# A two-block transformer on one core: the sine-table work of layer 0 split and moved, and the filler matmuls of the mix loop moved from step 15 to step 14

## Chip, core and metric

One Trainium2 chip, one of its cores. The metric is device microseconds from start to end of one execution, the median of several executions. The engines are TensorE (PE), VectorE (DVE), ScalarE (ACT), GpSimd (POOL) and the DMA queues that SyncE (SP) and ScalarE issue.

## What is computed

Two small transformer stacks run one after the other on the same 512 tokens of width 1024. The change touches only the first one, whose two layers are:

```python
for l in range(DEPTH):                      # DEPTH = 2
    h = rms_norm(x, g_mix_norm[l]);  z = h @ w_in[l]
    q_lat, kv_lat, k_rope = z[..., :256], z[..., 256:384], z[..., 384:416]
    uv, pin = z[..., 416:928], z[..., 928:]
    a  = mla_mixer(q_lat, kv_lat, k_rope, positions, ...)   # 4 heads, causal softmax, rotary part of 32
    gm = sgu_mixer(uv, ...);  po = pool_mixer(pin, ...)
    mix = concat([rms_norm(a), rms_norm(gm), rms_norm(po)])
    x = x + mix @ w_out[l]
    h = rms_norm(x, g_ffn_norm[l])
    x = x + (silu(h @ w_gate[l]) * (h @ w_up[l])) @ w_down[l]

def apply_rope(x, positions):
    ang = positions * inv_freq              # reduced by multiples of 2 pi in the kernel
    cos, sin = cos(ang), sin(ang)
    return concat([x1 * cos - x2 * sin, x2 * cos + x1 * sin])
```

The second stack has a gated convolution layer and a dilated-attention layer, each with a squared-ReLU MLP and a gate at the end; it uses the same sine and cosine tables (the upper 64 rows hold its frequencies).

## The kernel before

Everything is held transposed, with channels on the 128 partitions and the 512 tokens along the free axis. Weights stream from memory in 225 slabs of 128 x 2048 floats. SP loads a slab into one of two stage buffers, POOL splits it into a high part and a low part, and PE multiplies in three products (high by high, low by high, high by low: lines 665 to 667), so that the result has nearly the precision of fp32. The program is a list of phases written out by hand; within a phase the order on each engine is the order of the code, and semaphores tie the engines together.

A phase called mix is one layer of the first stack up to `w_out`. PE's order at its start, with the names that matter:

- Slab 0 and slab 1 give PSUM banks 0 and 1 (query latents) and banks 2 and 3 (key-value latents, raw rotary keys). In layer 0 the sum of squares of `x` is also made there; ACT takes its root (`root`) and DVE its reciprocal, `rstd` (`finish_norm`).
- `turn_rstd` transposes `rstd` into bank 6 (line 921). DVE copies one column of each block out (`columns_of_rstd`, line 2039) and so frees bank 6.
- Slab 2 is multiplied with the tokens on the partitions, one quarter `c` of the tokens at a time, 24 matmuls each. Inside `c == 1`, PE takes bank 6 (`take(p, 6)`) and makes four narrow sums (`narrow_sum`, line 940): 8 small matmuls each that add ACT's squares of the latents (`narrow_square`, line 1547) over the channels.
- Slab 3 raises the latents to queries, keys and values, and from there a long chain of small operations on DVE leads to the first scores.

In layer 0, DVE also prepares the rotary tables between `finish_norm` and `columns_of_rstd`: `angles` multiplies positions by frequencies, finds the nearest multiple of 2 pi and subtracts it in four parts. ACT's `tables` waits for it (`angle_ready`), then takes sine, absolute value and sine again; it stands in ACT's order ahead of the square of bank 2. Layer 1 has neither.

Later in the phase is the mix loop: 16 steps, four heads by four blocks of 128 query tokens. At loop turn `t`, PE makes the scores of step `t` and transposes the probabilities of step `r = t - 2` (line 1100), for which DVE has multiplied by the reciprocal of the row sum (line 2237). `busy_work` puts matmuls whose result nobody reads (line 710) ahead of the wait at steps 10 and 15. After the loop come the first six products of `w_out` (`out_part`), the last head's values (line 1067), and the spreading of a norm (`spread_norm`, line 718), which goes on to the rest of the `w_out` products.

Of the kernel before, what the change touches and what calls it, by code (L numbers as in the profile page):

```python
# [142 lines left out]
def two_pi_parts():  # L143

    parts, rest = [], 2 * math.pi
    for _ in range(3):
        unit = 2.0 ** (math.floor(math.log2(rest)) - 7)
        parts.append(math.floor(rest / unit) * unit)
        rest -= parts[-1]
    return parts + [rest]  # L150
# [29 lines left out]
def build(nc, a):  # L180

    ctx = ExitStack()
    with ctx:
# [194 lines left out]
        def col(name, i=0):  # L378
            c = COLUMN_AT[name] + i
            return cols[:, c:c + 1]  # L380

        def gcol(c, rows=P):
            return cols[0:rows, c:c + 1]

        def tile_end(ph, j):


            slab, tile = ph
            return (tile_done, tile + j // 2 + 1) if j % 2 == 0 else (slab_done, slab + j // 2 + 1)
# [272 lines left out]
        def _(pe):  # L662
# [16 lines left out]
            def take(p, b):  # L679

                at_least(pe, drained[b], p.drain[b] + used[b])
                used[b] += 1
# [24 lines left out]
            def busy_work(b, n):  # L707

                for _ in range(n):
                    pe.matmul(ps[:, b, :], xh[:, 0, 0:P], xh[:, 0, :], start=True, stop=True)  # L710
# [244 lines left out]
            def mix(p):  # L955
                L = p.layer
# [52 lines left out]
                def input_steps(j, steps):  # L1009

                    slab = s0 + 4 if j >= 2 else s0 + 5
                    for k in steps:
                        if k == 0:
                            if j % 2 == 0:
                                pe.wait_ge(slab_split, slab + 1)
                            take(p, j)
                        last = triple(ps[:, j, :], *blk(slab % 2, 2 * k + j % 2), xh[:, k, :], xl[:, k, :], k == 0, k == 7)
                        if k == 7:
                            last.then_inc(tile_done if j % 2 == 0 else slab_done, 1)
# [42 lines left out]
                def values(h):  # L1062
                    r = TOK * h + TOK - 1
                    pe.wait_ge(drained[6 + r % 2], turned_count(p, r))
                    take(p, h % 2)
                    for kb in range(TOK):
                        last = pe.matmul(ps[:, h % 2, kb * P:], vt1[:, kb, h * V_HEAD:(h + 1) * V_HEAD],  # L1067
                                         pt1[:, kb, kb * P:], start=kb == 0, stop=kb == TOK - 1)
                    last.then_inc(values_done, 1)
# [4 lines left out]
                for t in range(steps + 2):  # L1074
                    if t < steps:
                        h, i = divmod(t, TOK)
                        b = 4 + t % 2
                        if i == 0:
                            pe.wait_ge(head_ready, L * HEADS + h + 1)
                            fed = 7 - h % 2  # L1080
                            pe.wait_ge(drained[fed], p.drain[fed] + (2 if fed == 7 else 4) + h // 2)
                        take(p, b)
                        pe.matmul(ps[:, b, 0:(i + 1) * P], qk1[0:QK_HEAD, 2 * h, i * P:(i + 1) * P],  # L1083
                                  qk1[0:QK_HEAD, 2 * h + 1, 0:(i + 1) * P], start=True, stop=True).then_inc(scores_done, 1)
                    if t > TOK + 1 and t % TOK == 2:
                        values(t // TOK - 1)
                    if t in u_pairs:
                        j, k = u_pairs[t]
                        input_steps(j, (k, k + 1))
                    if t in between:  # L1090
                        between[t]()
                    if t >= 2:
                        r = t - 2
                        h, i = divmod(r, TOK)
                        b = 6 + r % 2
                        take(p, b)
                        busy_work(b, {10: 5, 15: 6}.get(r, 0))
                        pe.wait_ge(probs_ready, L * steps + r + 1)
                        for kb in range(i + 1):
                            last = pe.transpose(ps[:, b, kb * P:(kb + 1) * P], W[:, r % 3, kb * P:(kb + 1) * P], ident[:])  # L1100
                        last.then_inc(probs_turned, 1)
# [261 lines left out]
        def _(act):  # L1363
# [28 lines left out]
            def root(b, n, rows=P):  # L1392

                state["sums"] += 1
                act.wait_ge(summed, state["sums"])
                at_least(act, rstd_ready, state["sums"] - 1)
                act.activation(W[0:rows, ROOT, :], ps[0:rows, b, :], ACT.Sqrt, scale=1.0 / n,
                               bias=gcol(COLUMN_AT["eps"], rows)).then_inc(drained[b], 1)
# [53 lines left out]
            def split_tile(dst, src, scale=1.0):  # L1452
                act.activation(dst, src, ACT.Copy, scale=scale).then_inc(split_high, 1)
# [89 lines left out]
            def narrow_square(src, rows):  # L1543

                n = nsq[0]
                at_least(act, narrow_summed, n - 1)
                act.activation(W[rows, n % 2, :], src, ACT.Square).then_inc(narrow_squares, 1)
                nsq[0] += 1
# [5 lines left out]
            def mix(p):  # L1554
                L = p.layer
# [4 lines left out]
                for j in range(3):  # L1560
                    act.wait_ge(*tile_end((p.slab, p.tile), j))
                    narrow_square(ps[:, j, :], every)
                    gain = COLUMN_AT["q_lat"] + 2 * L + j if j < 2 else COLUMN_AT["kv_lat"] + L
                    split_tile(lath[:, j, :], ps[:, j, :], scale=gcol(gain))
                    if (L, j) == (0, 1):
                        root(7, D)
                        tables()
                act.wait_ge(*tile_end((p.slab, p.tile), 3))
                narrow_square(ps[rot, 3, :], rot)
                act.activation(kr[rot, :], ps[rot, 3, :], ACT.Copy, scale=cols[rot, COLUMN_AT["k_head"] + L:COLUMN_AT["k_head"] + L + 1]) \  # L1570
                    .then_inc(kr_raw, 1)

                for c in range(TOK):
                    if c % 2 == 0:
# [52 lines left out]
                for t in range(steps + 2):  # L1627
# [7 lines left out]
                    if t >= 2:  # L1635
                        r = t - 2
# [98 lines left out]
            def tables():  # L1735

                act.wait_ge(angle_ready, 1)
                act.activation(rope[:, 1, :], W[:, 2, :], ACT.Sin).then_inc(table_ready, 1)
                step(act.activation(W[:, 7, :], W[:, 2, :], ACT.Abs))
                step(act.activation(rope[:, 0, :], W[:, 7, :], ACT.Sin, scale=-1.0, bias=col("half_pi")))  # L1740
# [26 lines left out]
        def _(dve):  # L1767
# [280 lines left out]
            def mix(p):  # L2048
                L = p.layer
                sb0 = split_base_mix(p)  # L2050
                d = p.drain
                r, r2 = nar[:, 0:4], nar[:, 4:8]
# [7 lines left out]
                def low_of_latent(j):  # L2060
                    gain = COLUMN_AT["q_lat"] + 2 * L + j if j < 2 else COLUMN_AT["kv_lat"] + L
                    dve.wait_ge(split_high, sb0 + j + 1)
                    dve.scalar_tensor_tensor(out=latl[:, j, :], in0=ps[:, j, :], scalar=gcol(gain), in1=lath[:, j, :].bitcast(F32),
                                             op0=ALU.mult, op1=ALU.subtract).then_inc(drained[j], 1)
# [2 lines left out]
                low_of_latent(1)  # L2067
                if L == 0:
                    finish_norm(p)
                    angles()  # L2070
                columns_of_rstd(p, 6, r)
                step(tt(r2, r, r, ALU.mult))
                low_of_latent(2)
                dve.wait_ge(drained[2], d[2] + 1)
                dve.sem_inc(split_low, 3)
# [31 lines left out]
                for c in range(TOK):  # L2107
                    b = 4 + c // 2
# [34 lines left out]
                for h in range(HEADS):  # L2143
                    b = 7 - h % 2
# [240 lines left out]
                    dve.wait_ge(split_high, split_base_attn() + n + 1)  # L2385
                    tt(o2l[:, h, :], o2[:, h, :], o2h[:, h, :].bitcast(F32), ALU.subtract).then_inc(split_low, 1)

            def angles():

                dve.wait_ge(positions_landed, 32)  # L2390
                step(dve.tensor_copy(W[:, 3, :], kr_positions[:]))
                step(dve.tensor_scalar(W[:, 2, :], W[:, 3, :], col("inv_freq"), None, ALU.mult))
                magic = 1.5 * 2 ** 23
                step(dve.tensor_scalar(W[:, 3, :], W[:, 2, :], 1 / (2 * math.pi), magic, ALU.mult, ALU.add))
                step(dve.tensor_scalar(W[:, 3, :], W[:, 3, :], magic, None, ALU.subtract))
                for part in two_pi_parts():
                    step(dve.scalar_tensor_tensor(out=W[:, 2, :], in0=W[:, 3, :], scalar=-part, in1=W[:, 2, :],
                                                  op0=ALU.mult, op1=ALU.add))
                dve.tensor_scalar(W[:, 2, :], W[:, 2, :], 3.1415925, -3.1415925, ALU.min, ALU.max).then_inc(angle_ready, 1)
# [162 lines left out]
```

## Time and profile before

| | us |
|---|---|
| median of 3 runs | 2595.27 (2595.12 to 2596.69) |
| profiled execution, its own time | 2597.71 |
| span of the profile (first to last instruction) | 2595.9 |
| PE busy in the span | 2562.7 |
| POOL busy | 1814.7 |
| DVE busy | 1081.2 |
| ACT busy | 477.0 |

The profile is one execution. Its span is the time between the first and the last instruction; the time of the execution itself is slightly longer. An engine is idle wherever its rows in the timeline leave a gap, and a row's square bracket says how long the engine had been idle before it and which instruction ended the wait. PEclk is the TensorE clock that was granted, as a share of 2.4 GHz: 1.00 is 2.4 GHz and 0.50 is 1.2 GHz.

### The profile page before, as it was taken

The numbers are of one execution on the slowest core, as the hardware profiler recorded it, in microseconds if no ns is written. First come the engines' busy times: TensorE is split into PE (matmuls) and PEld (weight loads), VectorE is DVE, ScalarE is ACT, GpSimd is POOL, SyncE is SP. The second block draws the span as 40 slices with busy tenths as digits, with TensorE's granted clock in tenths as the row PEclk, the third lists the DMA queues.
The fourth block names the chain that finished last, engine by engine and source line by source line (L and its number), as shares of the span: only waits on it lengthen the run. The fifth ranks groups of instructions, "written<-read, shape, count | busy, mean of one in ns | idle before, by whom it ended". The sixth has DMA issues, their size and how long they took to land.

```text
span 2595.9 us, 31945 instructions
## 1 busy us (share of the span) xinstructions
PE 2562.7 (99%) x11846; PEld 2136.8 (82%) x11846; DVE 1081.2 (42%) x1741; ACT 477.0 (18%) x894; POOL 1814.7 (70%) x1825
## 2 busy tenths in 40 slices
PE   9999999999999999999999999999999999999998
PEld 8678888887788888888888888888988898888887
DVE  5753332036633320344530422696278344504315
ACT  4432111034421110201200002300310032100013
POOL 6637777666377776677786776687667777867764
PEclk8999999999999999999999999999999999999999
DMA  4112222231122222222222222222112203222221
GB/s 159 66 49 94 94 95 97 94 115 64 47 100 94 94 95 102 92 93 97 104 97 97 97 97 97 102 97 98 66 65 97 97 33 106 97 97 97 97 97 65
DMA packets 39440, 236.47 MB, mean 91 GB/s; under 512 B 4416, under 2 KB 8000, under 8 KB 12096
## 3 DMA queue, kind: packets, MB, share of 16 engines
q1 hardware_dynamic: 37488, 232.55, 25.8%
q10 hardware_dynamic: 1872, 2.80, 0.4%
q8 instruction: 56, 0.92, 0.1%
q14 instruction: 24, 0.20, 0.0%
HBM read 233.24 MB, written 2.10 MB: 91 GB/s over the span
## 4 chain that ended last, share of the span: by engine, by line
PE 94%; DVE 4%; ACT 1%; issue 1%; DMA 0%; SPq 0%; DVEq 0%; ACTq 0%
PE psum L665 30%; PE psum L666 29%; PE psum L667 29%; PE psum L1203 1%; PE psum L1067 1%; PE psum L1153 1%; PE psum L1185 0%; PE psum L1159 0%; PE psum L1083 0%; PE psum L940 0%; DVE qk L2033 0%; DVE qk L2034 0%; PE psum L695 0%; PE psum L1100 0%; DMA x_res<-in_x 0%
## 5 line engine op out<-in xcount | busy, mean ns | idle before, releaser
L528 POOL TENSOR_TENSOR w_low<-w_stage,w_high 128x512 fp32r<-128x512 f32 x836 | 1122.5, 1374 | 17.5
L523 POOL TENSOR_SCALAR w_high<-w_stage 128x512 fp32r<-128x512 f32 x836 | 554.1, 689 | 614.4 <-PE psum L667 612.7
L665 PE MATMUL psum<-x_high,w_high 128*128 128x512 f32 (+1 forms) x1680 | 657.0, 391 | 0.0
L667 PE MATMUL psum<-x_high,w_low 128*128 128x512 f32 (+1 forms) x1680 | 650.5, 387 | 0.0
L666 PE MATMUL psum<-x_low,w_high 128*128 128x512 f32 (+1 forms) x1680 | 650.4, 387 | 0.0
L666 PEld LDWEIGHTS psum<-x_low,w_high 128*128 128x128 f32 x1680 | 315.5, 188 | 66.8 <-issue 2.6
L665 PEld LDWEIGHTS psum<-x_high,w_high 128*128 128x128 f32 x1680 | 315.5, 188 | 66.7 <-issue 2.6
L667 PEld LDWEIGHTS psum<-x_high,w_low 128*128 128x128 f32 x1680 | 315.4, 188 | 64.2
L1855 DVE TENSOR_TENSOR psum<-psum,x_res 128x512 f32<-128x512 f32 x64 | 44.8, 700 | 459.1 <-PE psum L667 455.9
L665 PE MATMUL psum<-mlp_high,w_high 128*128 (+1 forms) x576 | 224.1, 389 | 0.0
L666 PE MATMUL psum<-mlp_low,w_high 128*128 (+1 forms) x576 | 224.1, 389 | 0.0
L667 PE MATMUL psum<-mlp_high,w_low 128*128 (+1 forms) x576 | 224.1, 389 | 0.0
L665 PE MATMUL psum<-attn_x_high,w_high 128*128 128x512 f32 x384 | 150.1, 391 | 0.0
L666 PE MATMUL psum<-attn_x_low,w_high 128*128 128x512 f32 x384 | 149.4, 389 | 0.0
L667 PE MATMUL psum<-attn_x_high,w_low 128*128 128x512 f32 x384 | 149.4, 389 | 0.0
L665 PE MATMUL psum<-ffn_high,w_high 128*128 (+1 forms) x352 | 136.9, 389 | 0.0
L666 PE MATMUL psum<-ffn_low,w_high 128*128 (+1 forms) x352 | 136.9, 389 | 0.0
L667 PE MATMUL psum<-ffn_high,w_low 128*128 (+1 forms) x352 | 136.9, 389 | 0.0
L1432 ACT ACTIVATE x_res<-psum 128x512 f32<-128x512 f32 x72 | 43.2, 600 | 487.4 <-DVE psum L1855 481.4
L666 PEld LDWEIGHTS psum<-mlp_low,w_high 128*128 128x128 f32 x576 | 108.1, 188 | 22.6
L665 PEld LDWEIGHTS psum<-mlp_high,w_high 128*128 128x128 f32 x576 | 108.1, 188 | 22.4
L667 PEld LDWEIGHTS psum<-mlp_high,w_low 128*128 128x128 f32 x576 | 108.1, 188 | 22.3
(322 smaller groups left out, 3435.8 us busy)
## 6 DMA issues: line engine op xcount, KB each, us to landing
w_stage<-in_wstream SPq DMA_DIRECT2D x213, 1024.0 KB, 4.9
w_stage<-in_wstream SPq DMA_DIRECT2D x12, 256.0 KB, 5.6
x_res<-in_x SPq DMA_DIRECT2D x8, 256.0 KB, 5.8
out_x<-x_res SPq DMA_DIRECT2D x16, 128.0 KB, 1.8
ple_proj<-in_p ACTq DMA_DIRECT2D x2, 512.0 KB, 3.7
inv_count_sb<-in_inv_count SPq DMA_DIRECT2D x1, 512.0 KB, 4.3
inv_count_sb<-in_inv_count ACTq DMA_DIRECT2D x1, 512.0 KB, 4.2
qk<-in_mask ACTq DMA_DIRECT2D x1, 306.0 KB, 2.8
```

The source lines that it names most:

```text
L523: last = pool.tensor_scalar(wh[:, s, part], stage[:, s, part], 1.0, 1.0, ALU.mult, ALU.mult)
L528: last = pool.tensor_tensor(wl[:, s, part], stage[:, s, part], wh[:, s, part].bitcast(F32), ALU.subtract)
L665: pe.matmul(out, wa, ra, start=start, stop=False)
L666: pe.matmul(out, wa, rb, start=False, stop=False)
L667: return pe.matmul(out, wb, ra, start=False, stop=stop)
L1067: last = pe.matmul(ps[:, h % 2, kb * P:], vt1[:, kb, h * V_HEAD:(h + 1) * V_HEAD], pt1[:, kb, kb * P:], start=kb == 0, stop=kb == TOK - 1)
L1153: last = pe.matmul(ps[:, k, at:at + P], qk2[:, 4 * g + h, n * P:(n + 1) * P], qk2[:, 12 + 4 * g + h, n * P:(n + 1) * P], start=True, stop= ...
L1203: last = pe.matmul(out, v2(g, c)[:, h * P:(h + 1) * P], pt2[:, k, n * P:(n + 1) * P], start=(k, n) == (0, 0), stop=(k, n) == (3, 3))
L1432: act.activation(x[:, m, :], ps[:, m, :], ACT.Copy)
L1855: tt(ps[:, m, :], ps[:, m, :], x[:, m, :], ALU.add).then_inc(x_summed, 1)
```

## The change

It has two independent parts. In layer 0, DVE's `angles` is cut in two: `turns` (four operations: positions, product, nearest multiple) stays in its place, and the rest (four subtractions and a clamp) now follows `columns_of_rstd` and the square of its result. ACT's `tables` moves behind the square of bank 2, its high part, the square of the raw keys and their copy to `k_rope`. In the mix loop of both layers, the fillers of step 15 (six) go to step 14 (seven).

```diff
@@ PE, mix loop
                         take(p, b)
-                        busy_work(b, {10: 5, 15: 6}.get(r, 0))
+                        busy_work(b, {10: 5, 14: 7}.get(r, 0))
                         pe.wait_ge(probs_ready, L * steps + r + 1)
@@ ACT, mix
                     if (L, j) == (0, 1):
                         root(7, D)
-                        tables()
                 act.wait_ge(*tile_end((p.slab, p.tile), 3))
                 narrow_square(ps[rot, 3, :], rot)
                 act.activation(kr[rot, :], ps[rot, 3, :], ACT.Copy, scale=cols[rot, COLUMN_AT["k_head"] + L:COLUMN_AT["k_head"] + L + 1]) \
                     .then_inc(kr_raw, 1)
+                if L == 0:
+                    tables()
@@ DVE, mix
                 if L == 0:
                     finish_norm(p)
-                    angles()
+                    turns()
                 columns_of_rstd(p, 6, r)
                 step(tt(r2, r, r, ALU.mult))
+                if L == 0:
+                    angles()
                 low_of_latent(2)
@@ DVE, the function cut in two
-            def angles():
+            def turns():
...
                 step(dve.tensor_scalar(W[:, 3, :], W[:, 3, :], magic, None, ALU.subtract))
+
+            def angles():
+
                 for part in two_pi_parts():
```

DVE in layer 0, from the reciprocal on; before:

```order
12 L1789 RECIPROCAL rstd<-work 128x512
13 L2391 CAST work<-k_rope 128x512
14 L2392 TENSOR_SCALAR work<-work,cols_sb 128x512
15 L2394 TENSOR_SCALAR work<-work 128x512
16 L2395 TENSOR_SCALAR work<-work 128x512
17 L2397 SCALAR_TENSOR_TENSOR work<-work 128x512 x4
18 L2399 TENSOR_SCALAR work<-work 128x512
19 L2039 COPY token_cols<-psum 128x4
20 L2072 TENSOR_TENSOR token_cols<-token_cols 128x4
21 L2063 SCALAR_TENSOR_TENSOR lat_low<-psum,cols_sb,lat_high 128x512
22 L2404 TENSOR_SCALAR rope<-rope,cols_sb 128x512
```

and with the change:

```order
12 L1790 RECIPROCAL rstd<-work 128x512
13 L2394 CAST work<-k_rope 128x512
14 L2395 TENSOR_SCALAR work<-work,cols_sb 128x512
15 L2397 TENSOR_SCALAR work<-work 128x512
16 L2398 TENSOR_SCALAR work<-work 128x512
17 L2040 COPY token_cols<-psum 128x4
18 L2073 TENSOR_TENSOR token_cols<-token_cols 128x4
19 L2403 SCALAR_TENSOR_TENSOR work<-work 128x512 x4
20 L2405 TENSOR_SCALAR work<-work 128x512
21 L2064 SCALAR_TENSOR_TENSOR lat_low<-psum,cols_sb,lat_high 128x512
22 L2410 TENSOR_SCALAR rope<-rope,cols_sb 128x512
```

The copy out of bank 6 (`token_cols<-psum`) moved ahead of five operations on 128x512.

ACT in layer 0, from the root of the mean square on; before:

```order
18 L1397 ACTIVATE work<-psum,cols_sb 128x512
19 L1738 ACT_TABLE_LOAD
20 L1738 ACTIVATE rope<-work 128x512
21 L1739 ACTIVATE work<-work 128x512
22 L1740 ACTIVATE rope<-work,cols_sb 128x512
23 L1547 ACTIVATE work<-psum 128x512
24 L1453 ACTIVATE lat_high<-psum,cols_sb 128x512
25 L1547 ACTIVATE work<-psum 32x512
26 L1570 ACTIVATE k_rope<-psum,cols_sb 32x512
27 L1576 ACTIVATE work,token_cols<-psum 128x256 x4
```

and with the change:

```order
18 L1397 ACTIVATE work<-psum,cols_sb 128x512
19 L1547 ACTIVATE work<-psum 128x512
20 L1453 ACTIVATE lat_high<-psum,cols_sb 128x512
21 L1547 ACTIVATE work<-psum 32x512
22 L1569 ACTIVATE k_rope<-psum,cols_sb 32x512
23 L1739 ACT_TABLE_LOAD
24 L1739 ACTIVATE rope<-work 128x512
25 L1740 ACTIVATE work<-work 128x512
26 L1741 ACTIVATE rope<-work,cols_sb 128x512
27 L1577 ACTIVATE work,token_cols<-psum 128x256 x4
```

The load of the sine's function table moved with the sines, behind the copy to `k_rope`.

PE at the end of the mix loop of layer 0 (layer 1 reads the same); `-` is before, `+` the change:

```order
 L1100 MATMUL psum<-ident,work 128x128
 L1083 MATMUL psum<-qk 128x512
-L1100 MATMUL psum<-ident,work 128x128 x5
-L710 MATMUL psum<-x_high 128x512 x6
-L1100 MATMUL psum<-ident,work 128x128 x4
+L1100 MATMUL psum<-ident,work 128x128 x2
+L710 MATMUL psum<-x_high 128x512 x7
+L1100 MATMUL psum<-ident,work 128x128 x7
 L665 MATMUL psum<-gate_pool_high,w_high 128x512
```

The two transposes of step 13 now have the fillers right behind them, and the three of step 14 and the four of step 15 follow with nothing between.

## Rows read from the trace of the kernel before

**Rows 1.** The page, part 1: busy time and share of the span.
```profile
PE 2562.7 (99%) x11846; PEld 2136.8 (82%) x11846; DVE 1081.2 (42%) x1741; ACT 477.0 (18%) x894; POOL 1814.7 (70%) x1825
```

**Rows 2.** Busy time by stretches of 1 and 5 us; third number from the end: PEclk.
```profile
38.00:39.00 1.00, 1.00 (x6) 1.00 (x6) 1.00 (x1) 1.00 (x2) 1.00 (x2) 0.56 0.00 0
55.00:56.00 1.00, 1.00 (x10) 1.00 (x9) 0.00 (x0) 0.00 (x0) 0.00 (x0) 0.91 0.00 0
137.00:138.00 1.00, 0.00 (x0) 0.00 (x0) 0.96 (x4) 1.00 (x4) 0.00 (x0) 0.55 0.00 0
143.00:144.00 1.00, 1.00 (x4) 0.74 (x3) 0.00 (x0) 1.00 (x3) 0.00 (x0) 0.53 0.00 0
144.00:145.00 1.00, 1.00 (x5) 0.68 (x4) 0.88 (x2) 0.96 (x2) 0.00 (x0) 1.00 0.00 0
125.00:130.00 5.00, 3.32 (x19) 2.66 (x20) 4.30 (x24) 2.44 (x6) 0.00 (x0) 1.00 0.56 210
669.00:670.00 1.00, 1.00 (x6) 0.78 (x5) 0.83 (x6) 0.34 (x1) 0.00 (x0) 0.79 0.00 0
```

**Rows 3.** The same view: slab 2's matmuls to slab 3's first, layer 0, then 1.
```profile
32.07:58.24 26.17, 23.39 (x128) 22.95 (x129) 11.48 (x20) 5.38 (x11) 9.12 (x8) 0.67 0.26 94
575.09:590.49 15.40, 15.40 (x131) 15.25 (x130) 4.65 (x13) 3.51 (x8) 7.37 (x8) 1.00 0.22 77
```

**Rows 4.** PE's timeline, layer 0: first narrow sum; first one of slab 3.
```profile
37.98 1.77 PE L940 MATMUL psum<-ones,work 128*128 128x1 f32 x8 [2.78 <-DVE token_cols L2039]
...
61.91 1.02 PE L940 MATMUL psum<-ones,work 96*128 96x1 f32 x8 [0.76 <-ACT work L1547]
```

**Rows 5.** DVE's timeline, layer 0, from the subtractions of 2 pi on.
```profile
32.28 4.17 DVE L2397 SCALAR_TENSOR_TENSOR work<-work 128x512 f32<-128x512 f32 x4
...
37.78 0.15 DVE L2039 COPY token_cols<-psum 128x4 f32<-128x4 f32 x1
...
47.11 0.68 DVE L2034 TENSOR_TENSOR k_rope<-work,k_rope 32x512 f32<-32x512 f32 x1
...
59.58 0.22 DVE L2095 TENSOR_TENSOR token_cols<-token_cols 128x4 f32<-128x4 f32 x1 [8.43 <-ACT work L1576]
```

**Rows 6.** ACT's timeline: sine in layer 0, a table load, raw keys in layer 1.
```profile
37.89 0.63 ACT L1738 ACTIVATE rope<-work 128x512 f32<-128x512 f32 x1 [11.90 <-DVE work L2399]
...
59.50 1.28 ACT L1552 ACT_TABLE_LOAD   x1
...
581.67 0.68 ACT L1570 ACTIVATE k_rope<-psum,cols_sb 32x512 f32<-32x512 f32 x1
```

**Rows 7.** POOL's timeline: the low part of slab 3 in layer 0.
```profile
36.00 5.45 POOL L528 TENSOR_TENSOR w_low<-w_stage,w_high 128x512 fp32r<-128x512 f32 x4
```

**Rows 8.** PE's timeline, end of layer 0's mix loop and what follows.
```profile
135.52 0.38 PE L1100 MATMUL psum<-ident,work 128*128 128x128 f32 x2
138.55 0.88 PE L1100 MATMUL psum<-ident,work 128*128 128x128 f32 x3 [2.64 <-DVE work L2237]
...
141.78 1.05 PE L1100 MATMUL psum<-ident,work 128*128 128x128 f32 x4
...
146.79 1.06 PE L718 MATMUL psum<-ident,window_a 128*128 128x128 f32 x8
```

**Rows 9.** The same view in layer 1: step 14, and the norm's spreading.
```profile
668.29 0.52 PE L1100 MATMUL psum<-ident,work 128*128 128x128 f32 x3 [2.64 <-DVE work L2237]
...
675.60 1.06 PE L718 MATMUL psum<-ident,window_a 128*128 128x128 f32 x8
```

**Rows 10.** DVE's timeline: probabilities of step 15; the norm's columns repeated.
```profile
138.51 0.49 DVE L2237 TENSOR_SCALAR work<-work,stat 128x512 f32<-128x512 f32 x1
...
141.28 0.43 DVE L2186 COPY window_a<-token_cols 128x512 f32<-128x512 f32 x1
```

**Rows 11.** PE's timeline, layer 0, earlier in the loop.
```profile
126.52 1.75 PE L710 MATMUL psum<-x_high 128*128 128x512 f32 x6
129.06 1.16 PE L718 MATMUL psum<-ident,work 128*128 128x128 f32 x8 [0.79 <-DVE work L2186]
```

## The prediction

> **What bounds the kernel now.** I read the page first. PE is busy for 2562.7 of the 2595.9 us [rows 1], so the kernel is PE's stream of matmuls, and it can get faster in only two ways without doing less: by PE waiting less (33 us are left in all), or by the same matmuls running at a higher clock. I therefore went through the span in stretches and looked for a granted clock below 1.00. Outside the last microseconds there are three places. The first begins at 38 us: the clock is 0.56 in that microsecond and comes back only within the one from 55 to 56 (0.91, so at 55.1). The second begins within 137 to 138 and lasts to 143.9 (0.53 in the one from 143 to 144, 1.00 in the next). The third begins at 669.6 (0.79 in that microsecond: 0.58 of it at 1.00, the rest at 0.50) [rows 2]. In each the level is 0.50, 1.2 GHz.
>
> Then I looked in PE's timeline for what stands before each fall. Each time it is an idle PE. Before the first it had waited 2.78 us to take bank 6, which DVE's copy of the turned `rstd` frees [rows 4]. Before the second and third it had waited 2.64 us for DVE's probabilities of step 14, once in each layer [rows 8, 9]. The two parts of the change touch just these three waits.
>
> **Part 1: layer 0, angles and tables.** In DVE's timeline the copy out of bank 6 starts at 37.78, because the four subtractions, which start at 32.28, and the clamp stand before it: 5.5 us [rows 5]. With the change the copy is next at 32.28 and takes 0.15 us. PE asks for bank 6 at 37.98 - 2.78 = 35.20, so the bank is then free with some 2.8 us to spare and the wait goes to nothing.
>
> What this stretch costs without the wait I need not guess, since layer 1 runs the same matmuls and narrow sums with no angles before them and at clock 1.00: from slab 2's first matmul to slab 3's first it takes 15.40 us, and in layer 0 it takes 26.17 [rows 3]. The difference, **10.8 us**, is the term: 2.8 of it the wait, 8.0 the half clock over the 17 us after it. PE would reach slab 3 at 32.07 + 15.40 = 47.47.
>
> This needs four covers. (a) The squares of bank 2 and bank 3 must be ready for the third and fourth narrow sum. In the old order they stood behind the sines, which began at 37.89 [rows 6]; now they stand as in layer 1, where the stretch has no wait. Were `tables` left ahead of them, this edit would leave the third sum waiting for the sines. (b) Slab 3 must be split by 47.47; POOL finishes it at 36.00 + 5.45 = 41.45 [rows 7]. (c) The five displaced DVE operations now end near 32.4 + 1.0 (my allowance for the short square behind the copy) + 5.5 = 39, and the low part of bank 2 right after; slab 3's matmuls need it at 47.47. (d) The tables are late next. In layer 1 the copy to `k_rope` ends at 582.35, 7.26 us after slab 2's first matmul [rows 3, 6], which is 39.3 here. Then come the table load, 1.28 us, and three ACT operations like the sine's 0.63 [rows 6]: about 42.6. DVE's rotation of the raw keys is four operations like its last one of 0.68 [rows 5], so it ends near 45.4, and four or five tiny ones follow: 46.4. In the old trace the first operation that needs the next thing, ACT's squares of slab 2's result, started 1.34 us after slab 3's first matmul (59.58 against 58.24) [rows 3, 5]; that is 48.8 now. DVE is free 2.4 us earlier, so I cost this at nothing. Without the cover, every microsecond of lateness would go one for one into the DVE chain toward the first scores.
>
> The table load's row shows 1.28 us and its sine could follow at once. The Trainium skill (ScalarE: Activation LUTs, What ACT_TABLE_LOAD costs) adds a drain of about 1.38 us to each switch of set; by it the tables come 1.4 us later and the cover shrinks to 1.0 us, still nothing on the path. In no row here do I see such a drain, and by either the sum stands.
>
> Behind slab 3's first matmul nothing is new: the chain of small DVE operations, POOL's splits and PE's wait of 0.76 us for ACT [rows 4] hang on each other and all move earlier together. That wait stays, for the root's table must still replace the sine's; if it went, 0.8 us more would be gained, the lower bound of this term. The other bound is that only the idle time goes: 2.8.
>
> **Part 2: the fillers.** Six fillers take 1.75 us at full clock [rows 11], so seven take about 2.0. PE's two transposes of step 13 end at 138.55 - 2.64 = 135.9 [rows 8]; the fillers fill to 137.8, and 0.75 us of idle time is left before step 14's transposes, which start at 138.55 as before, since DVE sets that. They cost nothing: PE would be idle. An idle time of 0.79 us in the same loop left the clock at 1.00 in all of 125 to 130 [rows 2, 11], and the fall at 137 came within the long gap. I take it that the clock stays.
>
> Step 15's probabilities are ready at 138.51 + 0.49 = 139.00 [rows 10], 0.6 us after step 14's; with the same delay to PE its transposes start at 139.15. Before, they started at 141.78, because six fillers stood ahead of them. From there to the spreading of the norm PE took 146.79 - 141.78 = 5.01 us, of which 2.2 (to 143.9) at half clock [rows 2, 8]; at full clock 3.9. So the spreading would start at 143.1 instead of 146.79: **3.7 us**. In layer 1 the same steps give 668.29 + 0.6 + 3.9 = 672.8 instead of 675.60 [rows 9]: **2.8 us** (less, as there the fillers ran mostly at full clock).
>
> Two covers. The norm's columns are repeated by 141.28 + 0.43 = 141.7 in layer 0 [rows 10], 1.4 us ahead of 143.1; in layer 1 the same distance holds. The last head's values need ACT's copy of step 15's transposes, some 0.6 us of work by a row of the same shape [rows 6], and six products of the fillers' size, about 1.4 us, lie between [rows 11]. What follows (squares of the heads, the gates' norm) hangs on the values and moves with them. Removing the fillers at step 15 uncovers only 0.1 to 0.3 us of waiting.
>
> **Sum.** 10.8 + 3.7 + 2.8 = 17.3 us. The profiled span would be 2595.9 - 17.3 = 2578.6. The profiled execution took 2597.71, 2.4 us over the median of the runs shown; the term is a difference, so I take it from the median: 2595.27 - 17.3 = **2578.0**. Little can eat it later: in the remaining 1900 us after layer 1's mix PE has almost no wait that an earlier start would lengthen.
>
> **The rivals.**
>
> A, the forecast: all three falls of the clock go. Chance 0.78.
>
> B, the clock falls at step 14 anyway, in one layer or both. The remaining gap is as long as one that did no harm, but this speaks from one row. Then from 139.15 to 5.4 us after PE resumed (138.55 to 143.9 before) the work runs at half clock: 4.8 us, of which 2.4 are lost. One layer: 2580.4; both: 2582.8. The Trainium skill (TensorE: Matmul & The Clock Gate, Part 1) says that the gate's window is free-running and that the point of transition varies with where it lies; by it a short gap may cost in one execution and not in another, and part 1 shifts this place by 10.8 us. In this trace the two equal gaps of 2.64 us did differ: one fall came within the gap, the other 1.3 us after it [rows 2, 8, 9]. Chance 0.10.
>
> C, layer 0 keeps its low clock in slab 2 although the wait is gone, say because the narrow sums are thin work right after the start. Then only 2.8 + 6.5 are gained: 2586.0. Layer 1's clock of 1.00 over the same work speaks against it. Chance 0.05.
>
> D, the change takes effect but does not shorten the kernel: a later stage, such as POOL's splitting at 70% [rows 1], sets the pace and PE waits there for what it gained. Then 2595. PE's 99% speak against it. Chance 0.03.
>
> E, the slower side: the clock falls before step 14 and, with no fillers behind the gap, the thin work there (transposes, values, norms) does not bring it back, as narrow sums kept it low for 17 us at 38 us. Each such stretch costs half its length. Two of 17.3 us eat the whole gain; from 22.5 us each the kernel is slower by over 0.2%; at twice the length seen, 34 us each, it takes 2578.0 + 34 = 2612. Against it: between the narrow parts lie dense products. Chance 0.02.
>
> Another 0.02 is for what I don't see.
>
> **How the numbers follow.** About 0.2% (5.2 us) is what a measurement of this kernel can tell from no change. A, B and C are faster, with half of the unseen: 0.94. Same 0.03 (D), slower 0.03 (E and the rest). The range goes down from 2578.0 by the 0.8 us and by 1.2 for the spread of the runs to 2576.0, and up to both layers of B, 2583.0. It leaves out C, D, E and a little of A, under 0.2.
>
> **What the changed profile would show.** The first narrow sum of layer 0 at about 35.0 with no wait; slab 3's first matmul near 47.5; no stretch below 1.00 before 130 us. At step 14 a gap of about 0.8 us behind seven fillers, clock 1.00, and the transposes of steps 14 and 15 some 0.6 us apart. The spreading of the norm 14.5 us earlier in layer 0, and 17.3 us earlier in layer 1. I am wrong if the fourth narrow sum or slab 3 waits, if DVE's rotation of the raw keys ends after 48, or if PEclk falls near 127 or 655.

## The result, and the profile after

The changed kernel takes 2582.15 us (median of 5 runs, 2580.16 to 2582.49) against 2596.23 for the kernel before (5 runs, 2595.12 to 2596.69): a ratio of 0.9945, with an interval of 0.993 to 0.9959, so 14.1 us less. A second measurement of the same two kernels, below, gave 15.0 us less. The forecast was 2578.0 in a range of 2576.0 to 2583.0. The profiled execution took 2580.91 us with a span of 2579.1, against 2597.71 and 2595.9: one execution against the other, 16.8 us less.

First the page's busy times of the changed kernel, to be read beside [rows 1]. PE has two matmuls more, one filler in each layer; the other engines have the same work.

```profile
PE 2551.0 (99%) x11848; PEld 2125.6 (82%) x11848; DVE 1081.0 (42%) x1741; ACT 476.7 (18%) x894; POOL 1814.5 (70%) x1825
```

PE makes the two additional matmuls and is still busy for 11.7 us less. So 11.7 of the 16.8 us are matmuls at a higher clock, and the rest is waiting. Next PE's timeline of the changed kernel, the rows that answer to [rows 3, 4, 8, 9] (start, duration, engine, line, operation; the bracket is the idle time before the row and what ended it).

```profile
34.87 0.95 PE L940 MATMUL psum<-ones,work 128*128 128x1 f32 x8
36.83 0.95 PE L940 MATMUL psum<-ones,work 128*128 128x1 f32 x8
38.80 0.95 PE L940 MATMUL psum<-ones,work 128*128 128x1 f32 x8
40.50 1.05 PE L940 MATMUL psum<-ones,work 32*128 32x1 f32 x8
50.99 1.02 PE L940 MATMUL psum<-ones,work 96*128 96x1 f32 x8 [0.76 <-ACT work L1547]
...
124.97 1.85 PE L710 MATMUL psum<-x_high 128*128 128x512 f32 x7
127.77 1.31 PE L1100 MATMUL psum<-ident,work 128*128 128x128 f32 x7 [0.95 <-DVE work L2240]
132.45 1.06 PE L718 MATMUL psum<-ident,window_a 128*128 128x128 f32 x8
...
653.83 1.31 PE L1100 MATMUL psum<-ident,work 128*128 128x128 f32 x7 [0.93 <-DVE work L2240]
658.52 1.06 PE L718 MATMUL psum<-ident,window_a 128*128 128x128 f32 x8
```

None of the four narrow sums waits, where the first had waited 2.78 us. The seven fillers end at 126.82 and leave 0.95 us. Then seven transposes run in one piece (three of step 14, four of step 15), and the spreading of the norm starts 4.68 us after the first of them in layer 0 and 4.69 in layer 1. Before it was 146.79 - 138.55 = 8.24 and 675.60 - 668.29 = 7.31 [rows 8, 9].

The same places by windows (length, then busy time of PE, PEld, DVE, ACT and POOL, the granted clock, the share and rate of DMA):

```profile
31.90:47.32 15.42, 15.42 (x128) 15.27 (x129) 11.51 (x20) 6.55 (x12) 9.18 (x8) 1.00 0.47 164
127.00:128.00 1.00, 0.23 (x2) 0.24 (x3) 0.93 (x5) 0.68 (x2) 0.00 (x0) 1.00 0.00 0
653.00:654.00 1.00, 0.17 (x1) 0.17 (x2) 0.93 (x5) 0.74 (x2) 0.00 (x0) 1.00 0.00 0
```

From slab 2 to slab 3 it is 15.42 us where it was 26.17 [rows 3], at a clock of 1.00. The microseconds that hold the remaining gap are at 1.00 too; the clock falls only in the last microseconds, as before.

DVE's timeline of the changed kernel shows the covers, to be read beside [rows 5]:

```profile
32.11 0.16 DVE L2040 COPY token_cols<-psum 128x4 f32<-128x4 f32 x1
32.73 4.81 DVE L2403 SCALAR_TENSOR_TENSOR work<-work 128x512 f32<-128x512 f32 x4
37.58 1.40 DVE L2405 TENSOR_SCALAR work<-work 128x512 f32<-128x512 f32 x1
38.89 0.74 DVE L2064 SCALAR_TENSOR_TENSOR lat_low<-psum,cols_sb,lat_high 128x512 fp32r<-128x512 f32 x1
41.15 0.49 DVE L2410 TENSOR_SCALAR rope<-rope,cols_sb 128x512 f32<-128x512 f32 x1 [1.52 <-ACT rope L1739]
44.73 0.68 DVE L2035 TENSOR_TENSOR k_rope<-work,k_rope 32x512 f32<-32x512 f32 x1
...
48.66 0.22 DVE L2098 TENSOR_TENSOR token_cols<-token_cols 128x4 f32<-128x4 f32 x1 [2.27 <-ACT work L1577]
```

The copy out of bank 6 starts at 32.11. The subtractions and the clamp follow it and end at 38.98, inside a stretch in which PE waits for none of them. The rotation ends at 45.41, five tiny operations follow, and DVE then waits 2.27 us for ACT. ACT's timeline of the same stretch, beside [rows 6]:

```profile
39.19 1.28 ACT L1739 ACT_TABLE_LOAD   x1
40.49 0.63 ACT L1739 ACTIVATE rope<-work 128x512 f32<-128x512 f32 x1
41.02 0.61 ACT L1740 ACTIVATE work<-work 128x512 f32<-128x512 f32 x1
41.67 0.72 ACT L1741 ACTIVATE rope<-work,cols_sb 128x512 f32<-128x512 f32 x1
```

The load ends at 40.47 and the sine starts at 40.49. The Trainium skill (ScalarE: Activation LUTs, What ACT_TABLE_LOAD costs) adds a drain of about 1.38 us to each switch of set; the trace does not agree, for there is no such time between the two rows.

### The profile page after: what moved, and what is told of

It is laid out like the page before. It is cut to its first block, busy times and chain, and to the rows that moved or that the text cites. A ratio compares the mean times of both kernels' runs of the same rounds, so it can differ in the third digit from the quotient of the medians.

```text
span 2579.1 us, 31950 instructions
## 1 busy us (share of the span) xinstructions
PE 2551.0 (99%) x11848; PEld 2125.6 (82%) x11848; DVE 1081.0 (42%) x1741; ACT 476.7 (18%) x894; POOL 1814.5 (70%) x1825
## 4 chain that ended last, share of the span: by engine, by line
PE 94%; DVE 4%; POOL 1%; issue 1%; ACT 0%; DMA 0%; SPq 0%; DVEq 0%; POOLq 0%; ACTq 0%
PE psum L665 30%; PE psum L667 30%; PE psum L666 30%; PE psum L1203 1%; PE psum L1067 1%; PE psum L1153 1%; POOL w_low L513 1%; PE psum L1159 0%; PE psum L1185 0%; PE psum L1083 0%; DVE qk L2034 0%; DVE qk L2035 0%; PE psum L695 0%; POOL w_high L511 0%; PE psum L940 0%
## 5 line engine op out<-in xcount | busy, mean ns | idle before, releaser
L528 POOL TENSOR_TENSOR w_low<-w_stage,w_high 128x512 fp32r<-128x512 f32 x836 | 1122.2, 1374 | 17.4
```

Of the source, the lines that this page charges most:

```text
L528: last = pool.tensor_tensor(wl[:, s, part], stage[:, s, part], wh[:, s, part].bitcast(F32), ALU.subtract)
```

## Experiments

The runs were made in three sessions, each on another chip, and each run is compared with the kernel before in its own session. So the differences can be set side by side, and the times themselves only within a session. "Less" is against the median of before in the same session: 2595.93 us in the first (again, part1, part2, gapfill), 2596.09 in the second (before_2, before_3, nofill, tables_first), 2597.36 in the third (gapfill13, part1_nofill, fill11, nofill_2).

**The changed kernel again**, unedited.

> The changed kernel once more, for a second trace and five more times. Theory V (the idle time of 0.9 us left before step 14 sometimes still lowers the clock, so that executions differ): the times fall in two groups about 2 us apart, the longer ones with a mean clock 0.001 lower, and a trace of a longer one shows a stretch at 0.50 that begins near step 14 of a layer. Rival W (the spread is as in the kernel before, from the first and last microseconds): traces show 1.00 at step 14 in both layers, and the difference stands before the first or behind the last slab. Both expect a median between 2580 and 2582.5.

2580.91 us (5 runs, ratio 0.9942, 0.9928 to 0.9956), 15.0 us less. Its trace has 15.44, 4.69 and 4.69 us at the three places and no low clock before the last microseconds. The five times lie within 0.8 us of each other, so the two groups of theory V did not appear here.

**Part 1 alone.** The changed kernel with the fillers of before:

```diff
-                        busy_work(b, {10: 5, 14: 7}.get(r, 0))
+                        busy_work(b, {10: 5, 15: 6}.get(r, 0))
```

> Part 1 alone (layer 0's angles cut in two, tables behind the raw keys; fillers still at step 15). Forecast: 10.8 us less than before, slab 3's first matmul near 47.5, no clock below 1.00 before 120 us, both falls at step 14 still there. Rival C (the low clock of layer 0 stays without the wait): 2.8 us less.

2586.12 us (5 runs, 0.9962, 0.9949 to 0.9976), 9.8 us less. The execution profiled is the fastest of the five, 2584.24. Its windows, layer 0's slab 2, layer 0's step 14 and layer 1's step 14:

```profile
31.48:46.88 15.40, 15.40 (x132) 15.25 (x129) 12.89 (x21) 6.55 (x12) 9.36 (x8) 1.00 0.47 162
128.00:129.00 1.00, 1.00 (x5) 0.76 (x5) 0.83 (x6) 0.27 (x1) 0.00 (x0) 0.80 0.00 0
655.00:660.00 5.00, 3.95 (x20) 3.22 (x21) 4.15 (x19) 2.94 (x8) 0.00 (x0) 1.00 0.00 0
```

And PE's timeline in layer 1:

```profile
656.05 0.52 PE L1100 MATMUL psum<-ident,work 128*128 128x128 f32 x3 [2.65 <-DVE work L2240]
656.32 1.63 PE L710 MATMUL psum<-x_high 128*128 128x512 f32 x6
...
661.77 1.06 PE L718 MATMUL psum<-ident,window_a 128*128 128x128 f32 x8
```

The wait of 2.65 us at step 14 stands here as before in both layers. In layer 0 the clock falls behind it (0.80 in the microsecond from 128), in layer 1 it stays at 1.00, and the spreading comes 5.72 us after the transposes, where [rows 9] give 7.31. So an idle time of this length makes the clock fall in one place and not in the other, with the same code.

**Part 2 alone.** The kernel before with the moved fillers:

```diff
-                        busy_work(b, {10: 5, 15: 6}.get(r, 0))
+                        busy_work(b, {10: 5, 14: 7}.get(r, 0))
```

> Part 2 alone (seven fillers ahead of step 14 instead of six ahead of step 15, layer 0's angles as before). Forecast: 3.7 + 2.8 = 6.5 us less than before, clock 1.00 at step 14 in both layers, the fall at 38 us unchanged. Rival B (the clock falls at the shortened gap too): 1.7 to 4.1 us less.

2591.18 us (11 runs, 0.9982, 0.9973 to 0.9991), 4.75 us less. The window from slab 2 to slab 3 is as in [rows 3]:

```profile
31.92:58.10 26.18, 23.40 (x128) 22.96 (x129) 11.48 (x20) 5.37 (x11) 9.13 (x8) 0.67 0.27 94
```

The two places at step 14 take 4.68 and 4.69 us, as in the changed kernel. The parts add: 9.8 + 4.75 = 14.55, where 14.1 and 15.0 were measured for both together.

**Is part 1's gain the wait or the clock?** The kernel before, with fillers in the wait for bank 6, so that the wait is as long but PE is not idle in it:

```diff
                             if k == 0:
+                                if L == 0:
+                                    busy_work(5, 11)
                                 take(p, 6)
```

> The kernel before, with eleven filler matmuls into bank 5 ahead of the take of bank 6 in layer 0: the wait for DVE's copy stays (2.8 us, of which the fillers cover 2.5), only the idle time of PE goes. If the forecast's split is right (2.8 us for the wait, 8.0 us for the clock), the clock stays at 1.00 after 38 us and the kernel is 8 us faster than before. If the low clock comes from the thin narrow sums and not from the idle time, the clock falls all the same and the time is that of before.

2590.07 us (11 runs, 2588.57 to 2597.61; 0.9982, 0.9973 to 0.9991), 5.9 us less by the medians; the ratio, in which the few long runs weigh more, comes to 4.7. The execution profiled took 2592.72. PE's timeline:

```profile
35.16 2.68 PE L710 MATMUL psum<-x_high 128*128 128x512 f32 x11
38.12 1.05 PE L940 MATMUL psum<-ones,work 128*128 128x1 f32 x8 [0.28 <-DVE token_cols L2041]
...
40.19 0.95 PE L940 MATMUL psum<-ones,work 128*128 128x1 f32 x8
```

and its windows:

```profile
40.00:41.00 1.00, 1.00 (x11) 1.00 (x11) 0.00 (x0) 1.00 (x2) 1.00 (x2) 1.00 0.00 0
41.00:42.00 1.00, 1.00 (x8) 1.00 (x8) 0.74 (x1) 0.88 (x3) 0.61 (x1) 0.71 0.06 16
51.00:52.00 1.00, 1.00 (x7) 1.00 (x7) 0.00 (x0) 0.00 (x0) 0.00 (x0) 0.67 0.00 0
```

Only 0.28 us of idle time is left, and the clock falls all the same, at 41.4, after two narrow sums, and is back at 51.7. I had expected it to stay. The stretch takes 23.08 us, 3.1 less than in before with the wait as long, because the clock is low for 10.2 us instead of 17. So the clock is worth something apart from the wait, but this trace does not show all 8.0 us of it. With 13 fillers the picture was no better.

```diff
-                                    busy_work(5, 11)
+                                    busy_work(5, 13)
```

> As gapfill, with thirteen fillers (about 3.0 us of matmuls against 2.8 of wait), so that PE has no idle time at all ahead of the narrow sums and takes bank 6 about 0.2 us late. If the 0.28 us of idle time left in gapfill was what let the clock fall among the narrow sums, the clock stays in every execution: 7.8 us faster than before, near 2588.2, and a spread of 2 us like that of the changed kernel. If the thin narrow sums alone do it when they fall at a bad time, times again spread from 2588 to 2597 and the trace may show a fall after 38.

2590.11 us (7 runs, 2587.66 to 2597.39; 0.9974, 0.9963 to 0.9986), 7.25 us less. In its profiled execution, 2596.48, DVE's copy came late and left 1.19 us of waiting before the first narrow sum at 38.85; the clock fell at 39.7. The runs of both kernels spread over 9 to 10 us, and those near 2588 fit a clock that stayed. No trace of these two kernels shows that, so it is an inference.

**The kernel before, twice more**, unedited, for the spread of its places.

> The kernel before once more, for a second trace. Theory P (the same idle time lowers the clock in one execution and not in another): the waits are again 2.8 us ahead of the narrow sums and 2.6 us at step 14 of each layer, but the clock falls at other distances from them, or at one of them not at all, and the span differs by 1 to 3 us accordingly. Rival Q (the falls are fixed to the program): clock and edges as in the first trace, 38.1 to 55.1, 137.1 to 143.9, 669.6 to 673.

> The kernel before a third time, as before_2: by theory P another set of falls, by Q the same.

The first took 2598.27 us (span 2596.5) and shows slab 2 to slab 3 and the two places at step 14 as in the rows of before: 26.16, 8.28, 7.31 us. The second took 2596.36 (span 2594.6). Its windows:

```profile
31.87:56.45 24.58, 21.80 (x128) 21.36 (x129) 11.48 (x20) 5.38 (x11) 9.13 (x8) 0.72 0.29 100
40.00:41.00 1.00, 1.00 (x9) 1.00 (x7) 0.08 (x1) 0.81 (x2) 1.00 (x2) 0.57 0.00 0
53.00:54.00 1.00, 1.00 (x7) 1.00 (x7) 0.00 (x0) 0.00 (x0) 0.00 (x0) 0.61 0.00 0
```

and its first two narrow sums on PE:

```profile
37.78 1.05 PE L940 MATMUL psum<-ones,work 128*128 128x1 f32 x8 [2.78 <-DVE token_cols L2039]
...
39.86 1.45 PE L940 MATMUL psum<-ones,work 128*128 128x1 f32 x8
```

The wait is the same 2.78 us, but the clock falls only at 40.1, 2.3 us after PE has resumed, and is back at 53.8. The low stretch is 13.7 us long instead of 17, and the place costs 1.6 us less. So the falls differ between executions of one kernel, as theory P had it.

**The fillers of step 15 taken out, nothing put in.**

```diff
-                        busy_work(b, {10: 5, 15: 6}.get(r, 0))
+                        busy_work(b, {10: 5}.get(r, 0))
```

> The kernel before with no fillers at step 15 and none at step 14 either. It splits part 2 in two. Theory: six fillers on the path cost about 1.3 us in each layer at full clock (1.4 us of matmuls, less the 0.1 us that step 15's probabilities come late), so this kernel is 2.5 us faster than before, and the rest of part 2's 4.8 us (2.3) is the clock kept by the fillers ahead of step 14; the wait of 2.6 us stays. Rival E's idea (without dense work behind the gap the clock stays low for long): slower than before by several us, the low stretch longer than 7 us.

2596.09 us (11 runs, 2592.41 to 2598.74; 0.9998, 0.9989 to 1.0007): no change, where I had expected 2.5 us less; the interval reaches down to 2.9 us less. In the profiled execution PE waited 4.09 us for bank 6 instead of 2.78:

```profile
39.09 1.37 PE L940 MATMUL psum<-ones,work 128*128 128x1 f32 x8 [4.09 <-DVE token_cols L2039]
```

The edit touches nothing there, and it hides the edit in this trace. So the same kernel was looked at once more.

> The kernel nofill once more, for a second trace: it was as fast as before where 2.5 us less was expected. If the low clock lasts longer without the fillers' dense work behind the gap, step 14 to the spreading of the norm takes over 7 us in a layer in which the clock fell; if the first trace's late copy out of bank 6 (4.1 us of wait instead of 2.8) was chance, this one has 2.8 again.

2597.16 us, span 2595.4. The wait for bank 6 is 2.77 us here, so the longer one was chance. PE's timeline in layer 1:

```profile
667.20 1.73 PE L1100 MATMUL psum<-ident,work 128*128 128x128 f32 x7 [2.64 <-DVE work L2237]
...
671.28 3.13 PE L1067 MATMUL psum<-probs_t,v_tok 128*128 128x512 f32 x8
674.25 1.06 PE L718 MATMUL psum<-ident,window_a 128*128 128x128 f32 x8
```

From transposes to spreading it is 6.80 us in layer 0 and 7.05 in layer 1, where before has 8.24 and 7.31: 1.4 and 0.3 us less. In nofill's first trace it is 7.00 and 5.65: 1.2 and 1.7 less. The work runs partly or wholly at half clock behind the same 2.64 us of waiting. So these two traces show 1.7 and 2.9 us less at the two places together, and the medians of the session none; whether the removal alone is worth nothing or the 2.5 us expected the runs leave open.

**Is the move of ACT's tables needed?** Part 1 alone, with `tables` back at its old place:

```diff
                         root(7, D)
+                        tables()
...
-                if L == 0:
-                    tables()
```

> Part 1 with DVE's angles cut in two, but ACT's tables left ahead of the square of bank 2. The first narrow sum has no wait, but the third waits for the square behind the three sine operations: about 3 us near 38. If that wait costs only itself, 10 - 3 = 7 us less than before; if it lowers the clock as the old wait did, up to nothing is left: 0 to 3 us less. If ACT's place in the change is of no importance, 10 us less, as part 1.

2592.84 us (11 runs; 0.9989, 0.998 to 0.9998), 3.25 us less, so about 6.5 of part 1's 9.8 us are lost. PE's timeline:

```profile
37.30 0.95 PE L940 MATMUL psum<-ones,work 128*128 128x1 f32 x8
...
42.05 1.87 PE L940 MATMUL psum<-ones,work 128*128 128x1 f32 x8 [2.63 <-ACT work L1547]
```

and its windows:

```profile
41.00:42.00 1.00, 0.00 (x0) 0.00 (x0) 0.00 (x0) 0.97 (x3) 0.78 (x1) 0.55 0.00 0
135.00:141.00 6.00, 5.84 (x28) 4.50 (x29) 4.68 (x19) 2.76 (x5) 0.00 (x0) 1.00 0.00 0
```

The first sum is free, but the third waits 2.63 us for ACT's square, which stands behind the sines. The clock falls inside that wait, at 41.1, and the stretch takes 22.47 us. The second window is step 14 of layer 0: there the clock stays at 1.00 behind 2.64 us of waiting, as in layer 1 of part1. Cutting `angles` without moving `tables` moves the stall; that is cover (a) of the prediction, shown.

**Is part 2's gain the removal, or the filled gap?** The changed kernel with no filler at step 14 or 15:

```diff
-                        busy_work(b, {10: 5, 14: 7}.get(r, 0))
+                        busy_work(b, {10: 5}.get(r, 0))
```

> The changed kernel with the seven fillers of step 14 left out (none at step 15 either). Against part1 it takes six fillers off the path, against the changed kernel it leaves the clock to fall in the wait of 2.6 us. If the fillers ahead of step 14 are what makes part 2 worth more than taking fillers away, this stands with part1 (2586) or between it and the changed kernel (2581): 2583 to 2587. If taking fillers off the path were all of part 2: 2581.

2585.62 us (5 runs; 0.9957, 0.9943 to 0.997), 11.7 us less than 2597.36. The changed kernel has 14.1 and 15.0 less, and fill11 (next, on the same chip) 15.0: so filling the gap gains about 3 us, and no run of the one kernel (2584.48 to 2586.8) reaches those of fill11 (2580.95 to 2582.89). Against part 1 alone, which is 9.8 us less, the removal without a fill gains up to 1.9 us; the intervals of the two overlap. The trace has 6.20 and 6.19 us at step 14, with a fall in both layers, against 4.68 with the gap filled, 3.0 us in both layers together. PE's timeline in layer 1:

```profile
656.90 1.55 PE L1100 MATMUL psum<-ident,work 128*128 128x128 f32 x7 [2.65 <-DVE work L2240]
...
663.09 1.06 PE L718 MATMUL psum<-ident,window_a 128*128 128x128 f32 x8
```

**Would filling the whole gap gain the rest?**

```diff
-                        busy_work(b, {10: 5, 14: 7}.get(r, 0))
+                        busy_work(b, {10: 5, 14: 11}.get(r, 0))
```

> The changed kernel with eleven fillers instead of seven, which fill the 0.95 us that PE still waits before step 14. If the idle time left never lowers the clock: 2581 as the changed kernel, the wait at step 14 gone from the rows of the waits, every other row the same. If it lowers it in the longer executions (2582.3 against 2580.5): a median of 2580.5 and a spread below 1 us.

2582.39 us (5 runs, 2580.95 to 2582.89; 0.9942, 0.9928 to 0.9955): 15.0 us less, as the changed kernel's second measurement. The places are 4.68 and 4.68 us with no idle time before them, so the 0.95 us that the seven fillers leave costs nothing. But the execution profiled, 2582.89, shows something new in layer 1's slab 2. PE's timeline there:

```profile
567.92 0.95 PE L940 MATMUL psum<-ones,work 128*128 128x1 f32 x8
...
569.62 1.05 PE L940 MATMUL psum<-ones,work 32*128 32x1 f32 x8
```

and its windows:

```profile
569.00:570.00 1.00, 1.00 (x10) 0.86 (x9) 0.93 (x3) 0.27 (x1) 0.00 (x0) 1.00 0.56 98
571.00:572.00 1.00, 1.00 (x6) 1.00 (x6) 0.75 (x5) 0.00 (x0) 0.00 (x0) 0.50 1.02 434
574.00:575.00 1.00, 1.00 (x9) 1.00 (x9) 0.00 (x0) 0.00 (x0) 0.00 (x0) 0.83 0.00 0
```

No narrow sum waits, and yet the clock falls behind the fourth, from 570.9 to 574.3. From layer 0's spreading to layer 1's first score this trace takes 476.93 us and the changed kernel's 475.40: 1.5 us. Of the 14 traces, this one and part1_nofill's (572.3 to 575.7) have such a fall; the other twelve do not. Both were taken on the same chip, so whether it is the chip or chance the runs leave open.

**All traces on one scale.** The places are the stretch from slab 2's first matmul to slab 3's first in layer 0, and the stretch from step 14's transposes to the spreading of the norm in each layer. If the three places are the whole story, each trace's span follows from the changed kernel's 2579.1 by adding what its places take beyond 15.42, 4.68 and 4.69 us, and 1.5 where layer 1's narrow sums fall.

| trace | slab 2 to 3, layer 0 | step 14, layers 0 and 1 | sum over 2579.1 | span over 2579.1 |
|---|---|---|---|---|
| before | 26.17 | 8.24, 7.31 | 16.9 | 16.8 |
| before_2 | 26.16 | 8.28, 7.31 | 17.0 | 17.4 |
| before_3 | 24.58 | 8.40, 7.33 | 15.5 | 15.5 |
| part2 | 26.18 | 4.68, 4.69 | 10.8 | 10.3 |
| gapfill | 23.08 | 7.31, 5.73 | 11.3 | 11.8 |
| tables_first | 22.47 | 5.73, 7.28 | 10.7 | 11.2 |
| part1 | 15.40 | 7.32, 5.72 | 3.7 | 3.3 |
| part1_nofill | 15.40 | 6.20, 6.19 and 1.5 | 4.5 | 4.4 |
| fill11 | 15.43 | 4.68, 4.68 and 1.5 | 1.5 | 2.0 |
| nofill | 27.42 | 7.00, 5.65 | 15.3 | 15.2 |
| nofill_2 | 26.13 | 6.80, 7.05 | 15.2 | 16.3 |
| gapfill13 | 25.98 | 7.31, 7.31 | 15.8 | 15.6 |
| again | 15.44 | 4.69, 4.69 | 0.0 | -0.1 |

The two last columns agree within 0.5 us in all but one row (nofill_2, 1.1), so little happens elsewhere in the span.

## Why the prediction was right, and where it was off

**The mechanism held, point by point.** All three waits and all three falls are gone. The first narrow sum came at 34.87 (forecast about 35.0), slab 3's first matmul at 47.32 (47.5), the norm's spreading 14.34 us earlier in layer 0 (14.5) and 17.08 in layer 1 (17.3). The wait of 0.76 us for ACT stayed, as said. The four covers held: (a) is shown by tables_first; (b) slab 3's first matmul had no wait before it; the displaced DVE operations ended at 38.98 (39); the rotation at 45.41 (45.4), and the next thing was needed at 48.66 (48.8), so 2.3 us were spare. Of the 17.1 us 0.3 are given back in the last ten microseconds: the last sum there (L858) starts 17.06 us earlier but takes 0.98 us where it took 0.58, since the clock at the end falls sooner (at 2568.5 against 2587.9), and the last row of turns (L865) starts at 2571.75 against 2588.50, 16.75 earlier; hence the 16.8 of the spans.

**The sum of 17.3 us was too large for a median.** The forecast lies 4.1 us below the measured 2582.15, near the edge of its range. Of these, 1.0 is where it starts: the median of three runs was 2595.27, that of five is 2596.23. The other 3.2 are 17.3 us forecast against 14.1 measured, and the step that failed there is "the term is a difference, so I take it from the median". It is a difference between one execution of before and a kernel without falls, and that execution had all three falls, and long ones: 2597.71 us, near the top of what the kernel before takes (2593.79 to 2598.62 over the runs of all sessions) and 1.5 over its median. From that execution's own time the same sum gives 2597.71 - 17.3 = 2580.4, and the changed kernel's profiled execution took 2580.91: 0.5 us are left to the terms (the places at step 14 gave 6.2 us for 6.5, and 0.3 was given back at the end). The last 1.2 us are that the changed kernel's median lies over its own profiled execution; why stays open, as the next paragraph says.

Other executions of before lose less: before_3 has 24.58 us in slab 2 where [rows 3] have 26.17, and part 1 alone has 5.72 us at step 14 of layer 1 where [rows 9] give 7.31. For part 2 the average over traces shows it: the seven with six fillers at step 15 average 14.4 us for both places at step 14, 5.0 over the changed kernel's 9.4, and the medians gave 4.75 where I had 6.5. For part 1 it does not: the six traces in which the stretch of slab 2 has the old code average 26.1 us, 10.7 over the changed kernel's, and the medians gave 9.8 where I had 10.8. Both forecasts lie inside the intervals of these runs, 2.3 to 7.0 us for part 2 and 6.2 to 13.2 for part 1.

**"Each time it is an idle PE" was not the whole condition.** In gapfill the clock fell with 0.28 us of idle time, in fill11 and part1_nofill with none before the narrow sums of layer 1. What stands before each of these falls is narrow sums, the thin work that rival C had in mind, only not where C looked: in layer 0 the five traces without a wait there show no fall. That the thin work is the cause is likely but not shown, for the same rows stand in twelve traces without a fall. Where it happens with no idle time it costs 1.5 us, not 8. It accounts for 1.5 of the 2.0 us between the fill11 execution profiled and the changed kernel's at 2580.91; for the changed kernel's own executions near 2582.3 it is a likely cause but not shown, since both of its profiled executions, 2580.91 and 2580.79, are without it.

**Rivals.** B: the gap of 0.95 us (forecast 0.75) lowered the clock in none of the six places traced (both layers of the changed kernel, twice, and of part 2 alone), and fill11, without that gap, is no faster. Longer gaps do differ from one execution to the next, as B had it: with a wait of 2.64 or 2.65 us at step 14 the clock fell in 17 of 20 places, in ten traces. The Trainium skill (TensorE: Matmul & The Clock Gate, Part 1) says that the gate's window is free-running, so that the point of transition varies with where it lies; the traces agree that the point varies, for behind the same idle time of 2.6 to 2.8 us the fall came within the wait, up to 2.3 us behind it, or not at all, but none shows the reason. D and E did not occur. PE stayed at 99%, with no new wait of size.

**Part 2's working** did not part the fillers from the clock. The rows now do. Where the clock stays at 1.00 behind the wait, with six fillers at step 15, the place takes 5.72 or 5.73 us (part1, gapfill, tables_first); with the gap filled it takes 4.68. So the six fillers cost 1.0 us in each layer, and 4.1 of the 6.2 us between before (8.24 + 7.31) and the changed kernel (4.68 + 4.69) are the clock. Taking the fillers away without filling the gap does not secure the rest: the medians show nothing alone and up to 1.9 us beside part 1.

## What to carry to other kernels

Where a trace shows a low granted clock, price the whole low stretch and not the wait before it, and look at the same code in another layer, which may run without the fall. But the size of a fall is a draw for each execution: take such terms from the time of the execution in which they were read, or look at two or three executions of before. Fillers help where they stand in the idle time itself, ahead of the wait. Where thin work follows, taking away the wait is the surer way: gapfill gained 5.9 us and part 1 gained 9.8, of which 2.8 are the wait itself, and gapfill's runs spread over 9 us where part 1's spread over 3.

## What the runs showed of the hardware

- The same code with the same idle time (2.64 or 2.65 us at step 14) lowered the clock in layer 0 and not in layer 1 of one execution (part1), and in both layers of another (before). Over ten traces it fell in 17 of 20 such places; behind 0.95 us or less at step 14 it fell in none of eight.
- Around narrow sums (8 matmuls of 128x1 each, between dense products) the clock fell with no idle time at all in 2 of 14 traces (fill11 and part1_nofill, layer 1), for 3.4 us each, and in layer 0 of gapfill, after 0.28 us of idle, for 10.2 us.
- DVE's copy in layer 0 came late in two executions although nothing ahead of it was edited on DVE: it started at 38.88 us in nofill and 38.65 in gapfill13, where it is 37.78 in before. In nofill PE's wait there was 4.09 us instead of 2.78, and slab 3's first matmul came at 59.31 instead of 58.24, 1.1 us later.
